# The adaLN modulation of a fused two-block kernel, summed and turned in three groups instead of sixteen chunks

## What is computed

```python
# block 1
c_act = silu(c)                                   # [1, 1024]
mod = c_act @ w_ada + b_ada                       # 6 x 1024: sh1, sc1, ga1, sh2, sc2, ga2
u = rmsnorm(x, g_norm1) * (1 + sc1) + sh1
h = x + ga1 * hybrid_mixer(u)                     # projections, gated linear attention, conv
u2 = rmsnorm(h, g_norm2) * (1 + sc2) + sh2
h = h + ga2 * moe(u2)                             # 32 experts, top 2
modf = c_act @ w_ada_f + b_ada_f                  # 2 x 1024
x = rmsnorm(h, g_final) * (1 + scf) + shf
# block 2: attention, pooling and SSD branches, w_o, then a conv FFN, final rmsnorm
```

## Time and profile before

| | |
|---|---|
| median of 3 runs | 1471.61 us |
| the profiled execution, its own time | 1468.99 us |
| its span | 1467.2 us |
| PE busy | 1226.6 us (84%) |
| DVE busy | 672.8 us (46%) |
| ACT busy | 456.0 us (31%) |
| bytes read from HBM | 372.02 MB, 257 GB/s over the span |
| TensorE clock granted, mean | 0.911 of full speed |

### The profile page before, as it was taken

How to read it: one execution, slowest core, us unless ns; L and a number is a source line. 1 busy time by engine, 2 the same in 40 slices (tenths; PEclk the granted TensorE clock), 3 DMA queues, 4 the chain that set the end, 5 groups by cost and what they waited for, 6 DMA issues and landing times.

```text
span 1467.2 us, 20287 instructions
## 1 busy us (share of the span) xinstructions
PE 1226.6 (84%) x8730; PEld 969.2 (66%) x8730; DVE 672.8 (46%) x1103; ACT 456.0 (31%) x651; POOL 1.9 (0%) x15
## 2 busy tenths in 40 slices
PE   6989989998956657566675689999998989899998
PEld 4779887796423223132231389899997979899986
DVE  2647996553200000000000355356656777668974
ACT  1533333533000000000000343334545553554453
POOL 0000000000000000000000000000000000000000
PEclk8899999999979788798788789899998989999999
DMA  9785641996999999999999566343543335345552
GB/s 333 276 299 191 222 144 42 361 337 240 415 419 419 420 419 421 420 419 420 420 420 419 206 195 190 125 125 113 166 152 122 116 115 174 110 162 174 200 201 87
DMA packets 166151, 374.48 MB, mean 255 GB/s; under 512 B 5782, under 2 KB 118824, under 8 KB 141352
## 3 DMA queue, kind: packets, MB, share of 16 engines
q1 hardware_dynamic: 165888, 369.55, 67.8%
q0 software_dynamic: 144, 3.54, 0.7%
q10 hardware_dynamic: 24, 0.03, 0.0%
HBM read 372.02 MB, written 4.62 MB: 257 GB/s over the span
## 4 chain that ended last, share of the span: by engine, by line
PE 57%; DMA 22%; DVE 11%; SPq 5%; ACT 4%; issue 3%; DVEq 0%; ACTq 0%
PE bank L565 31%; DMA arena<-in_w 11%; DMA above<-in_w 8%; SPq L2485 4%; PE bank L1160 4%; DVE arena L1191 4%; PE bank L847 4%; DVE fine L1183 3%; ACT fine L1955 2%; DVE arena L1183 2%; PE bank L877 2%; PE bank L562 2%; PE bank L593 2%; ACT arena L1955 1%; DMA arena<-in_w_in 1%
## 5 line engine op out<-in xcount | busy, mean ns | idle before, releaser
L565 PE MATMUL bank<-fine 128*128 128x256 f32 x4656 | 587.5, 289 | 27.7 <-DVE fine L1183 17.0
L565 PEld LDWEIGHTS bank<-fine 128*128 128x128 f32 x4656 | 577.0, 196 | 37.2 <-issue 33.6
L1183 DVE TENSOR_TENSOR fine<-arena,fine 128x1024 fp32r<-128x1024 f32 (+2 forms) x263 | 300.4, 1167 | 179.7 <-ACT fine L1955 170.1
L1955 ACT ACTIVATE fine<-arena 128x1024 fp32r<-128x1024 f32 (+2 forms) x279 | 267.0, 984 | 181.6 <-PE bank L565 100.3
L1955 ACT ACTIVATE arena<-bank 128x256 f32<-128x256 f32 (+2 forms) x161 | 73.6, 484 | 566.7 <-PE bank L860 181.0
L847 PE MATMUL bank<-arena 128*32 128x512 f32 x640 | 126.1, 810 | 53.3 <-DMA arena<-in_w 34.0
L1183 DVE TENSOR_TENSOR arena<-arena,bank 128x512 f32<-128x512 f32 x8 | 8.4, 1054 | 290.7 <-PE bank L847 290.7
L847 PE MATMUL bank<-above,arena 128*32 128x512 f32 x384 | 78.9, 747 | 54.7 <-issue 25.0
L1955 ACT ACTIVATE arena<-arena 128x512 f32<-128x512 f32 (+6 forms) x94 | 63.2, 703 | 153.2 <-DVE arena L1183 62.0
L1191 DVE SCALAR_TENSOR_TENSOR arena<-arena 128x256 f32<-128x256 f32 (+3 forms) x262 | 107.6, 481 | 1.1 <-ACT arena L1955 0.8
L847 PEld LDWEIGHTS bank<-arena 128*32 128x32 f32 x640 | 31.3, 142 | 110.5 <-issue 110.4
(11 more groups left out here) (162 smaller groups left out, 775.0 us busy)
## 6 DMA issues: line engine op xcount, KB each, us to landing
arena<-in_w SPq DMA_DIRECT2D x120, 1024.0 KB, 26.9
above<-in_w SPq DMA_DIRECT2D x72, 1024.0 KB, 26.5
arena<-in_w_in SPq DMA_DIRECT2D x62, 1024.0 KB, 5.5
arena<-in_w_ada SPq DMA_DIRECT2D x24, 1024.0 KB, 8.9
arena<-in_ffn_w_up SPq DMA_DIRECT2D x22, 1024.0 KB, 5.1
arena<-in_ffn_w_down SPq DMA_DIRECT2D x11, 1024.0 KB, 5.0
arena<-in_w_ada_f SPq DMA_DIRECT2D x8, 1024.0 KB, 12.7
arena<-in_w_gla_o SPq DMA_DIRECT2D x4, 1024.0 KB, 12.1
```

The lines of the kernel that those rows point to most:

```text
L565: ins = e.matmul(o, w[:, k, j * P:j * P + P], x[:, kt, :], start=start, stop=stop, skip_group_check=True)
L1183: return e.tensor_tensor(o, a, b, f)
L1955: return e.activation(o, i, f, bias=bias, scale=scale)
```

## The change

- The chunks form three groups, 0-3, 4-9 and 10-15. All sums of a group go to bank 7: chunk i of a group multiplies with a column window of `cz`, a buffer of zeros with silu(c) in column 5, so that its sums fall in row i of each 32-row strip. One copy, four matmuls against a 6-column `sel` and one add per group take the place of one copy and four matmuls per chunk. Group 0's copy stands after DVE's `norm_apply(0)`; group 1 is copied in level 2, turned in level 3, its `mod_of(1)` and `gain(1)` move from behind the layer norm into level 3; group 2 is copied by ACT before the squares of norm(1) and turned in the first quad, in bank 4.
- The first eight loads have eight slots and wait for nothing; the bias one-hot load, which shares a slot, now waits for `ada_sum[4]`. Chunks 10 and 11 are loaded between the gates pieces (f = 22 waits for the sums of f = 20) and summed in level 4 (the fifth), chunk 10 after the scores, chunk 11 after the pieces. Chunks 12 to 15 take the places that 10 to 13 had; nothing of the modulation stands behind `norm(1)` on PE.
- `make_first`: the first piece of u1, u2, u3 makes all products with the high part of x first, tile by tile as ACT writes it, and those with the low part last. At u1, ACT and DVE split q's first half ahead of the tiles and the second half between them, DVE writing the low parts of x later.
- `flush(1)` ahead of the wait for `decay_v["k", 0]` and ahead of the wait for `decay_v["kd"]`.

```diff
-        ada_slots = [..., arena[:, q_at:q_at + SLOT]]
+        ada_slots = [..., arena[:, q_at:q_at + SLOT],
+                     flat(v), scr[:, 0:SLOT], scr[:, SLOT:2 * SLOT], arena[:, q_at - SLOT:q_at],
+                     arena[:, early_at + SLOT:early_at + 2 * SLOT]]
...
             if f < 8:
-                return f % 4, ada_slots[f % 4], f - 4 if f >= 4 else None
+                return f, ada_slots[f], None
             if f < 20:
-                return (f - 8) % 3, ada_slots[(f - 8) % 3], f - 3 if f >= 11 else f - 4
-            return (f - 20) % 3, ada_slots2[(f - 20) % 3], f - 3 if f >= 23 else None
+                return (f - 8) % 3, ada_slots[(f - 8) % 3], f - 3 if f >= 11 else f - 8
+            if f < 24:
+                return (8, 2)[f % 2], ada_slots[(8, 2)[f % 2]], {20: None, 21: 19}.get(f, f - 2)
+            return (f - 24) % 3, ada_slots2[(f - 24) % 3], f - 3 if f >= 27 else None
+        ADA = (range(0, 4), range(4, 10), range(10, 16))
...
+            def make_first(p, half, bank):
+                name, ph = FACTOR[p.name], int(p.n >= PIECES1)
+                def products(kt, x, both, start=False, stop=False):
+                    parts = [shaped(w[:, 0:4 * p.width], 4, p.width) for w in w_parts[ph][(2 * p.n + kt // 4) % NU]]
+                    for j in range(p.width // P):
+                        for i, w in enumerate(parts[:1 + both]):
+                            ins = e.matmul(bank[:, j * 256:j * 256 + 256], w[:, kt % 4, j * P:j * P + P], x[ph][:, kt, :],
+                                           start=start and i + j == 0, stop=stop, skip_group_check=True)
+                    return ins
+                for kt in range(4 * half, 4 * half + 4):
+                    e.wait_ge(*x_hi_a[name, "tile", kt])
+                    products(kt, x_hi, True, start=kt == 0)
+                if half:
+                    for kt in range(KT):
+                        e.wait_ge(*x_lo_v[name, "tile", kt])
+                        ins = products(kt, x_lo, False, stop=kt == KT - 1)
+                        if kt % 4 == 3:
+                            ins.then_inc(*products_of.up((p.n, kt // 4)))
...
-                        ins = e.matmul(bank[32 * k:32 * k + 32, :], cact[:, kt:kt + 1].to_broadcast([P, 32]), slot[:, k, :],
-                                       start=f % 2 == 0, stop=f % 2 == 1, skip_group_check=True)
+                        ins = e.matmul(banks[7][32 * k:32 * k + 32, :], cz[:, kt, 5 - i:37 - i], slot[:, k, :],
+                                       start=f == 2 * ADA[g][0], stop=f == 2 * ADA[g][-1] + 1, skip_group_check=True)
...
+            def ada_to_mod(g, bank=None):
+                n = len(ADA[g])
+                e.wait_ge(*ada_row(g)[g])
+                bank = take(bank, mod_out, g) if bank else misc(mod_out, g)
                 for m in range(4):
-                    ins = e.matmul(banks[7][:, 4 * j + m:4 * j + m + 1], aacc[:, j % 2, m * P:m * P + P], sel,
-                                   start=True, stop=True)
-                ins.then_inc(*ada_mod.up(j))
+                    ins = e.matmul(bank[:, n * m:n * m + n], aacc[:, g % 2, m * P:m * P + P], sel[:, 0:n], start=True, stop=True)
+                ins.then_inc(*ada_mod.up(g))
...
             for li in range(7):
                 if li < 6:
+                    if li == 0:
+                        flush(1)
                     e.wait_ge(*decay_v["k", li])
...
-                if li < 4:
-                    ada_to_mod(6 + li)
+                if li == 3:
+                    ada_to_mod(1)
+                if li == 4:
+                    ada_sums(10)
                 for name in fill[done:done + LEVEL_PIECES[li]]:
                     advance(name, 1)
+                if li == 4:
+                    ada_sums(11)
                 if li == STATES_AT:
+                    flush(1)
                     e.wait_ge(*decay_v["kd"])
...
             norm(1)
-            ada_sums(14)
-            ada_to_mod(13)
-            ada_sums(15)
...
+            scale(0)
+            scale(1)
+            low_half()
+            scale(2)
+            scale(3)
+            low_half()
+            scale(4)
+            scale(5)
+            for k in range(4):
+                rest(k)
+            scale(6)
+            scale(7)
+            for k in range(4, KT):
+                rest(k)
...
             norm_rows(1, lambda pair: out_v["w_out", pair])
-            rows_ada(14)
-            rows_ada(15)
             e.wait_ge(*mod_out["am1"])
```

More of the change, by code:

```diff
@@ L443, in build @@
         out_written = [signal(f"out_written{i}") for i in range(4)]
-        ada_in = [signal(f"ada_in{i}") for i in range(4)]
+        ada_in = [signal(f"ada_in{i}") for i in range(9)]
         ring_in = [signal(f"ring_in{i}") for i in range(NS)]
@@ L550, in make @@
                 first = p.i == 0 and FIRST[FACTOR[p.name]] == p.name
-                if first and FACTOR[p.name] not in TILE_BY_TILE:
+                if first and FACTOR[p.name] in TILE_BY_TILE:
+                    make_first(p, half, bank)
+                    return
+                if first:
                     e.wait_ge(*x_lo_v[FACTOR[p.name], half])
@@ L555, in make @@
                         kt = 4 * half + k
-                        if first and j == 0 and FACTOR[p.name] in TILE_BY_TILE:
-                            e.wait_ge(*x_lo_v[FACTOR[p.name], "tile", kt])
                         o = bank[:, j * 256:j * 256 + 256]
@@ L1338, in vector_program, with scale @@
                         *h_in.up((tc, g)))
+            norm_apply(0, h)
             rows_ada(0)
-            rows_ada(1)
-            norm_apply(0, h)
-            rows_ada(2)
-            rows_ada(3)
-            advance("q", 1)
-            mod_of(0, 0, 16, col("b_ada", 0, 16))
+            mod_of(0)
             gain(0, "g_norm1", 8)
             e.wait_ge(*mod_out["am0"])
-            for k in range(KT):
+            def scale(k):
                 if k % 4 == 0:
@@ L1442, in vector_program @@
                     factors(li + 1)
-                if li < 3:
-                    rows_ada(7 + li)
+                if li == 2:
+                    rows_ada(1)
+                if li == 3:
+                    mod_of(1)
+                    gain(1, "g_norm2", 32)
                 for name in fill[done:done + LEVEL_PIECES[li]]:
@@ L1491, in vector_program @@
             tt(cacc, cacc, repeat(mu, 4), ALU.mult).then_inc(*lnorm_v.up("scaled"))
-            mod_of(1, 16, 24, col("b_ada", 16, 24))
-            gain(1, "g_norm2", 32)
             for tc in range(2):
@@ L2068, in norm_split, with rows_ada @@
                         *x_hi_a.up((name, "tile", k)))
[L2070 to L2074 removed]
+            def rows_ada(g):
+                e.wait_ge(*ada_sum[2 * ADA[g][-1] + 1])
+                e.wait_ge(*ada_mod[g - 2])
+                act(aacc[:, g % 2, :], banks[7][:, :], ACT.Copy).then_inc(*ada_row_a.up(g))
             e.wait_ge(*cols_in["first"])
[L2077 removed]
+            e.wait_ge(*fills["cz"])
+            act(cz[:, :, 5], col("c", 0, 8), ACT.Silu).then_inc(*cact_on.up(0))
             norm_rows(0, lambda pair: h_in[1, pair // 2])
[L2079 removed]
+            high_half()
             e.wait_ge(*mod_out["am0"])
[L2081 removed]
+            for k in range(KT):
+                if k == 4:
+                    high_half()
+                if k % 4 == 0:
+                    e.wait_ge(*normed[0, k // 4])
+                act(x_hi[0][:, k, :], sq[:, k, :], ACT.Identity, scale=am[:, k:k + 1], bias=mod[:, k:k + 1]).then_inc(
+                    *x_hi_a.up(("u1", "tile", k)))
             advance("q", 1)
@@ L2511, in sync_program @@
             load("v", 2)
-            load("gates", 8)
+            load("gates", 2)
             ada(10)
+            load("gates", 2)
+            ada(11)
+            load("gates", 4)
+            ada(12)
             load("pw", 2)
```

153 lines of the change are left out of this document (65 added, 88 removed).

## The result

The changed kernel takes 1446.76 us (median of 4 runs, 1444.22 to 1450.87), the kernel before 1470.86 us beside it (4 runs, 1469.76 to 1472.62). The ratio is 0.9838 with a 95% interval of 0.9811 to 0.9865: 24 us or 1.6% faster. The forecast was 1448.5 us, with a range of 1441 to 1462.

A forecast was written before the change was run, and what follows sets the result against it. The prediction took DMA transfers to bound the experts' stage, and PE, then DVE from level 2, the mixer. Terms A to G sum to -23.1 us, giving 1448.5 us on the median's scale, range 1441 to 1462.

The forecast's parts named there:

- A: Start of the kernel: eight load slots, one turning per group and the new order make the first products earlier; -5.2 us.
- B: Products ahead of the levels: the turnings of chunks 4 and 5 leave a PE that always has work; -2.0 us.
- C: Mixer levels 0 and 1: two flushed halves fill PE's idleness ahead of the first scores, two turnings go; -9.1 us.
- D: Mixer levels 2 to 6: flushed halves fill idleness ahead of the states' products, output starts at 239.9 to 241.7; -0.6 us.
- E: From the output products to norm(1): three turnings less on PE, with w_out's first weights no earlier; -2.3 us.
- F: From norm(1) to the first expert quad: ACT no longer waits for PE's sums, the router starts earlier; -2.5 us.
- The stream: Experts' weight loads: slot 8 waits for the first quad's products, so the stream gains A to F only, nothing more.
- The rivals of the stream: Experts' loads: gaining the idle 13.3 us, 1437.7 us, chance 0.04; or losing the backlog, a gap per slot, 1492, chance 0.04.
- G: Second block's and FFN's first products: they start earlier because ACT's high tile is ready before DVE's low one; -0.9 and -0.5 us.

The follow-up runs named there:

- the fifth experiment: The changed kernel with four slots instead of eight for the first eight modulation loads: 1451.42 us, ratio 0.9882.
- The first experiment: The changed kernel without the flush ahead of the first scores (level 0): 1455.79 us, ratio 0.9895.
- The second experiment: The changed kernel without the flush ahead of the states' products (the wait for decay_v kd): 1449.61 us, ratio 0.9841.
- The fourth experiment: The changed kernel with chunk 15's sums moved behind norm(1) and their copy behind ACT's squares: 1447.57 us, ratio 0.9840.
- the seventh experiment: The changed kernel with the expert loads of slot 3 and after held back until norm(1)'s sum is done: 1448.84 us, ratio 0.9857.
- the last experiment: The changed kernel with high parts first only for the mixer's first product, the experts' block's and FFN's as before the change: 1452.34 us, ratio 0.9865.
- the tenth experiment: The changed kernel with chunk 15's sums behind norm(1), their copy behind the squares, and no flush ahead of the states' products: 1448.11 us, ratio 0.9855.
- the eighth experiment: The changed kernel with three quarters of the matmuls of chunks 10 and 11's sums left out: 1449.09 us, ratio 0.9872.

## Why the forecast held, and where it didn't

The forecast for the median, 1448.5, is 1.7 us above the measured one. Stage by stage:

*A* was -5.2 and is -5.98, within its bounds. The first product stood 0.1 from where it was put. Behind it the clock decides: 48.5 was given for full clock and 52 for half of the products without it, and both occur, in one and the same code. Of the working the first line is in doubt: the gap in the DMA was put down to four slots (2.2 us), and the fifth experiment has four slots and no gap when the squares take 3.69 us.

*B*, -2.0, is -1.77: two turnings out of a PE that has no other pause.

*C*, -9.1, is -9.12. The first experiment shows 7.6 of it to be the flush; DVE and ACT follow as said. That it fits to 0.02 is luck in part: the term counts on full clock in level 0, and eight of the twelve executions with the flush lose it there for 1.5 us, which makes C -7.6.

*D* failed: -0.6 forecast, bounds up to +1.0, and +2.26 measured. The first part of the step was right: L706's successor starts 2.8 us late, with 2.7 to 4.4 forecast. What failed is "so the output starts at 239.9 to 241.7", 17.4 us behind L706 with the last masked scores. The masks came even earlier, 14.84 us behind L742, since the states' 24 products ran in 4.01 us instead of 6.41; but the output starts 21.04 behind it. The step counted DVE's work up to the masks and left out that PE comes to the output only behind two half pieces, of which the second has its low part behind the masks. In the kernel before, four half pieces (96 matmuls, 11.76 us) stood there without a wait, and L706 to output was 21.57, not 17.4: this could have been read. The second experiment puts 1.2 us of the miss on the flush; with the 48 matmuls back behind the states it is still 21.87.

*E*, -2.3, is -0.89, just outside its bound of -1.0. ACT's wait for w_out's weights stayed, as was said, and is the same to a hundredth:

```profile
295.16 2.96 ACT L1999 ACTIVATE fine<-arena 128x1024 fp32r<-128x1024 f32 x3 [6.11 <-DMA arena<-in_w_out]
```

6.11 us for 6.10. Whatever PE saved ahead of it was spent there. Behind it w_out's first product comes 0.7 us earlier within the stage, where 1.0 was forecast. Of the turning that stood behind that product, 0.98 us, only 0.2 are won, because PE now waits for the last load:

```profile
305.86 1.07 PE L630 MATMUL bank<-arena 128*32 128x512 f32 x8 [0.48 <-DMA arena<-in_w_ada_f]
```

So E was mis-sized: on the old scale that load lands at about 320.5 (305.86 and the 14.61 us by which the output is earlier), where the forecast had 318. The fourth experiment shows what is still in that stage, 2.1 us for one chunk's sums.

*F*, -2.5, is -4.02, at its bound. The router lost its clock in part behind 5.24 us without work (5.14 us for 16 products; 3.63 with sums in the gap, in the fourth experiment). What wasn't counted is the gather behind it, 1.6 us shorter at full clock. Other executions of the same code have it at 5.64, so F is -4.0 or -1.2 by the clock alone. The rule of the Trainium skill that the prediction names ("TensorE: Matmul & The Clock Gate", section "What's actually happening"), that activity releases the slow clock, agrees with the trace at the router; the -1.4 that the prediction drew from it for the whole stage did not come, as the gather made up for it in this execution.

*The stream* starts with slot 8 and not earlier, as said: the seventh experiment bears it out. The rivals of the stream, both of them, didn't happen: 451 us as before, so no slot pays a gap.

*G* was mis-sized: -0.9 and -0.5, together -1.4 with a bound of -1.9, and it is -4.4 from the last experts' products on. The first products themselves are 1.2 and 1.0 earlier (23.51 for 24.73 us behind the experts; 7.93 for 8.92 behind the FFN's norm). The other 2.2 follow from the order of the first products too, by the last experiment, but through the clock: 2.1 up to the layer norm of the second block and 1.5 from there to the FFN's norm, and 1.4 given back from the FFN's first product to the end.

So the sum, -23.1 for -24.8, is better than its terms: D and E miss by 4.3 to one side, F and G by 4.5 to the other. And the profiled execution is a lucky one: of the thirteen it alone has the early a1, full clock in level 0 and the gather at full clock together. With the loss in level 0 (1.5 us), as in eight of the twelve with the flush, its gain would have been 23.3 us; with the slow gather (2.8 us), as in seven of the twelve variants, 22.0; with both 20.5, and some 4 less again with a late a1. So B's and C's mechanisms are borne out and A's in the main, and that the sum hit to 2 us is luck in part.

## What to carry to other kernels

Ahead of an in-order engine's critical product, count every piece of filler that stands in front of it in the program, with the wait of each; the stall's length is set by the last operand of the last filler, not by the product's own inputs. Filling a wait with ready work pays in full where the engine has no pause behind it (level 0, 6.1 to 7.6 us), and costs where the next stage then lacks filler (the states, about 1 us). Moving a filler behind the product also moves what reads its result in order on the next engine: look there before calling the wait removed.

## What the runs showed of the hardware

- **The granted clock differs from execution to execution in the same code, in steps.** Over the thirteen profiled executions, of the changed kernel and its twelve variants, the norm's 16 squares at 11 us take 3.69 us in seven and 5.5 to 6.2 in six; the first a1 product stands at 48.1 to 50.6 in seven and at 52.2 to 52.9 in six; the 48 matmuls behind a1 take 6.0 us in eight and 7.2 to 7.5 in five; the 72 of level 0 (flush in place) 8.86 us in four and 10.3 to 10.4 in eight, so that from a1 to the taps of level 2 it is 87.6, 89.1 or 90.6 us; from norm(1) to the first quad 24.4 to 24.6 in five and 27.4 in five (with the sums behind the norm 23.0, 25.8 and 27.5). These add up to some 10 us between the best and the worst, and hide edits of 3 us in medians of 5 runs. The Trainium skill, "TensorE: Matmul & The Clock Gate", section "What's actually happening", says that the same kernel shows different counts of slow matmuls at its start from run to run; the traces agree, and show it at three places more in the middle of the program: behind a1 (a wait of 0.67 us ahead), in level 0 (2.10 us) and between norm(1) and the first quad (5.24 us ahead of the router).
- **Behind equal waits the clock may hold or fall.** After 2.10 us without work, the next 72 matmuls take 8.86 us in the changed kernel and 10.32 in the tenth experiment. Which it is behind the 2.78 us in the second block went with the order of products 280 us earlier: 3.78 us for 4 matmuls in the two kernels with the old order, 1.99 in the changed one, and from the second block's first product to the end the eleven other variants are as short as the changed one (612.6 to 613.6 us).
- **One strip of 32 columns costs what four cost:** 1.90 us for 4 matmuls in the eighth experiment, 1.93 for 16 in the changed kernel.
